# A two-block transformer kernel in split fp32: the order of small steps around its stage changes, and two placing tables moved to GpSimd

## The reference, cut to what matters

```python
# gated linear attention: decays from a low-rank gate
log_a = log_sigmoid(lr @ w_gate2 + b_gate) / 16
cum = cumsum(log_a) in chunks of 64;  last = cum[..., -1, :]
k_dec = k * exp(last - cum);  chunk_decay = exp(last)
state = chunk_decay * state + k_dec^T v;  o = q state

# mixture of experts: a group of 4 experts for each token, then the top 2 of the group
g_idx = argmax(x @ w_group + b_group)
within = top-2 softmax over the 4 experts of that group
y += combine[:, e] * ((silu(x @ w_gate[e]) * (x @ w_up[e])) @ w_down[e])

# differential attention, 8 heads
w = softmax(q1 k1^T * scale + bias) - lam * softmax(q2 k2^T * scale + bias)
o = rms_norm(w @ v) * (1 - lambda_init);  out = o @ w_out
```

## Time and profile before

| what | value |
|---|---|
| median of 3 runs | 1870.49 us (1869.71 to 1872.28) |
| the profiled execution's own time | 1868.49 us |
| its span, first to last instruction | 1866.7 us |
| TensorE busy | 1830.5 us (98%) |
| VectorE busy | 1302.3 us (70%) |
| ScalarE busy | 1013.4 us (54%) |
| GpSimd busy | 107.6 us (6%) |
| mean granted TensorE clock | 0.996 |

### The profile page before, as it was taken

The page is one execution under the profiler, slowest core; times in us unless marked ns, Lnnn a source line. Parts: engine busy times, 40 slices in busy tenths (PEclk is TensorE's granted clock), DMA queues, the critical chain, the costliest instruction groups (busy, mean ns, idle before and its releaser), DMA issues.

```text
span 1866.7 us, 21829 instructions
## 1 busy us (share of the span) xinstructions
PE 1830.5 (98%) x9112; PEld 1531.4 (82%) x9112; DVE 1302.3 (70%) x1333; ACT 1013.4 (54%) x1083; POOL 107.6 (6%) x101
## 2 busy tenths in 40 slices
PE   7999999999999999999999999999999999999998
PEld 6788888887978888887888888888888888888886
DVE  4579999987779899897554677655465546875544
ACT  6447777775646777774443374544344434735431
POOL 1020000001010000000000300100010003020000
PEclk9999999999999999999999999999999999999999
DMA  9447999996446999996555653655565556346541
GB/s 341 153 163 265 357 370 356 359 363 224 137 135 225 359 361 346 375 363 226 188 193 167 195 181 106 207 191 176 191 206 190 176 192 203 134 141 211 190 169 57
DMA packets 220170, 426.57 MB, mean 229 GB/s; under 512 B 7560, under 2 KB 28304, under 8 KB 220064
## 3 DMA queue, kind: packets, MB, share of 16 engines
q1 hardware_dynamic: 214256, 406.93, 63.3%
q0 software_dynamic: 5808, 18.17, 3.2%
HBM read 424.01 MB, written 1.06 MB: 228 GB/s over the span
## 4 chain that ended last, share of the span: by engine, by line
PE 92%; DVE 4%; ACT 2%; DMA 1%; issue 0%; POOL 0%; DVEq 0%; SPq 0%
PE ps L485 26%; PE ps L477 25%; PE ps L480 25%; DVE Wlo L426 2%; PE ps L596 2%; PE ps L469 1%; PE ps L470 1%; PE ps L2526 1%; PE ps L1306 1%; PE ps L1619 1%; PE ps L576 1%; PE ps L575 1%; PE ps L574 1%; ACT Whi L414 1%; PE ps L2427 1%; PE ps L2022 1%
## 5 line engine op out<-in xcount | busy, mean ns | idle before, releaser
L426 DVE TENSOR_TENSOR Wlo<-raw,Whi 128x2048 fp32r<-128x2048 f32 (+2 forms) x387 | 865.6, 2243 | 409.9 <-ACT Whi L414 409.2
L414 ACT ACTIVATE Whi<-raw 128x2048 fp32r<-128x2048 f32 (+2 forms) x393 | 736.0, 1878 | 474.9 <-PE ps L485 469.7
L485 PE MATMUL ps<-Whi,XTl 128*128 128x512 f32 (+2 forms) x1496 | 549.5, 377 | 0.0
L477 PE MATMUL ps<-Whi,XTh 128*128 128x512 f32 (+2 forms) x1368 | 521.0, 381 | 9.4 <-DVE Wlo L426 8.0
L480 PE MATMUL ps<-Wlo,XTh 128*128 128x512 f32 (+2 forms) x1368 | 514.8, 376 | 0.0
L485 PEld LDWEIGHTS ps<-Whi,XTl 128*128 128x128 f32 x1496 | 280.7, 189 | 50.6
L477 PEld LDWEIGHTS ps<-Whi,XTh 128*128 128x128 f32 x1368 | 258.4, 189 | 57.5 <-DVE Wlo L426 8.0
L480 PEld LDWEIGHTS ps<-Wlo,XTh 128*128 128x128 f32 x1368 | 258.4, 189 | 44.6 <-issue 0.3
L477 PE MATMUL ps<-Whi,hTh 128*128 128x512 f32 x352 | 137.8, 391 | 0.0
L485 PE MATMUL ps<-Whi,hTl 128*128 128x512 f32 x352 | 137.1, 390 | 0.0
L480 PE MATMUL ps<-Wlo,hTh 128*128 128x512 f32 x352 | 137.1, 389 | 0.0
(11 more groups left out here) (350 smaller groups left out, 1998.7 us busy)
## 6 DMA issues: line engine op xcount, KB each, us to landing
raw<-in_moe_w_gate SPq DMA_DIRECT2D x64, 1024.0 KB, 5.7
raw<-in_moe_w_up SPq DMA_DIRECT2D x64, 1024.0 KB, 6.4
raw<-in_moe_w_down SPq DMA_DIRECT2D x64, 1024.0 KB, 6.0
raw<-in_ffn_gate SPq DMA_DIRECT2D x44, 1024.0 KB, 5.1
raw<-in_ffn_up SPq DMA_DIRECT2D x44, 1024.0 KB, 5.1
raw<-in_ffn_down SPq DMA_DIRECT2D x40, 1024.0 KB, 5.0
raw<-in_w_in SPq DMA_DIRECT2D x18, 1024.0 KB, 5.2
raw<-in_a_w_in SPq DMA_DIRECT2D x10, 1024.0 KB, 13.2
```

Of the source, the lines that this page charges most:

```text
L414: act.activation(Whi[:, i % NS, 0:m * n], raw[:, i % NR, 0:m * n], ACT.Copy).then_inc(w_rounded, tick(w_rounded, "rounded", i))
L426: dve.tensor_tensor(Wlo[:, i % NR, 0:m * n], raw[:, i % NR, 0:m * n], h.bitcast(f32), ALU.subtract).then_inc(w_rest, tick(w_rest, "rest", i))
L477: pe.matmul(o, xh(k, t), h[:, q, :], start=k == first, stop=False)
L485: x = pe.matmul(o, xl(k, t), h[:, q, :], start=False, stop=k == end)
```

## The change

It has seven parts, none of which changes the number of instructions of TensorE.

1. In the gated linear attention `decays` and `line` change places, on TensorE and on ScalarE: `line` after v1's unit 0, `decays` after its unit 1.
2. In the router's end VectorE takes two of the four gathered parts, then the rest of the first up unit, then the other two parts. Before, it took all four and then the unit.
3. The placing tables of groups 2 and 3 are written by GpSimd, which waits for a new point `chosen` (the mask `gm` is done); VectorE no longer writes them.
4. At the experts' end the add of (group 3, t = 1, first half) goes behind the last `Ygl`, ahead of the overflow branch, and its stats go to the very end, behind the last add.
5. ScalarE copies two of the four parts of the bias table ahead of the turn of X and two behind it (layer 0).
6. In the attention's out product unit 2 takes an `early` callback: it waits for the high half of its input only, runs 8 matmuls, and then waits for the low half.
7. `flip(7)` comes ahead of `values(6)` on TensorE and ScalarE.

```diff
@@ outer_pe
-    def outer_pe(pe, v, name, ready, order=(0, 4), hold=3):
+    def outer_pe(pe, v, name, ready, order=(0, 4), hold=3, early=None):
...
-            use_unit(pe, js[i], t, bs[i % 2][t], xt_h, xt_l, ready, order[0], order[1] + 3)
+            use_unit(pe, js[i], t, bs[i % 2][t], xt_h, xt_l, ready, order[0], order[1] + 3, early=early if i == 2 else None)
@@ gla_pe and gla_act, job v1
             if z == 0:
+                line()
+            if z == 1:
                 decays()
-            if z == 1:
-                line()
@@ gather_two_dve
-    def gather_two_dve(dve, l, p):
-        for kg in range(4):
+    def gather_two_dve(dve, l, p, part=range(4)):
+        for kg in part:
@@ route_dve
-        dve.tensor_tensor(gm[:, :, :], gm[:, :, :], oh[:, :, :], ALU.mult).then_inc(dve_done, tick(dve_done))
+        dve.tensor_tensor(gm[:, :, :], gm[:, :, :], oh[:, :, :], ALU.mult).then_inc(
+            dve_done, tick(dve_done, "chosen", l))
...
-        gather_two_dve(dve, l, 0)
+        gather_two_dve(dve, l, 0, range(2))
         rest_units(dve, jobs["up", l, 0, 0][0])
+        gather_two_dve(dve, l, 0, range(2, 4))
@@ moe_pool
+        P = MAIN[l]
+        pool.wait_ge(*on("chosen", l))
+        for g in range(2, 4):
+            for t in range(2):
+                pool.tensor_scalar(Pm[:, t, g, :], cst[:, C_IOTA:C_IOTA + 128], rank[:, t, g:g + 1], gm[:, t, g:g + 1],
+                                   ALU.is_equal, ALU.mult).then_inc(pool_done, tick(pool_done, P.name, "P", g))
         overflow_pool(pool, l, pool.soon())
@@ moe_act
-            bias_table_act(act)
+            bias_table_act(act, range(2))
         round_units(act, last_unit(v + 1) + 2)
         x_turn_act(act, v + 1, 0)
+        if l == 0:
+            bias_table_act(act, range(2, 4))
@@ moe_dve
         route_dve(dve, l, v)
-        for g in range(2, 4):
-            place_dve(dve, P, g, rank, gm)
...
                     if z == 0 and hf == 1 and g == 3:
-                        for t in range(2):
-                            scatter_dve(dve, P, l, 3, t, 0)
-                            stats_dve(dve, t, 0)
+                        scatter_dve(dve, P, l, 3, 0, 0)
+                        stats_dve(dve, 0, 0)
+        scatter_dve(dve, P, l, 3, 1, 0)
         overflow_dve(dve, l, place)
-        for t in range(2):
-            scatter_dve(dve, P, l, 3, t, 1)
-            stats_dve(dve, t, 1)
-            if t == 0:
-                norm_a_dve(dve, v + 1, 0)
-                norm_b_dve(dve, v + 1, 0)
+        scatter_dve(dve, P, l, 3, 0, 1)
+        stats_dve(dve, 0, 1)
+        norm_a_dve(dve, v + 1, 0)
+        norm_b_dve(dve, v + 1, 0)
+        scatter_dve(dve, P, l, 3, 1, 1)
+        for hf in range(2):
+            stats_dve(dve, 1, hf)
@@ diff_pe
+        def o_early(pe, k, t):
+            if k % 4 == 0:
+                pe.wait_ge(*on("hi", "doT", k // 4, t))
...
-        for z in outer_pe(pe, 3, ("df", "out"), o_ready, hold=2):
-            if z == 0:
+        for z in outer_pe(pe, 3, ("df", "out"), o_ready, hold=2, early=o_early):
+            if z == 0:
+                flip(7)
                 values(6)
-                flip(7)
                 values(7)
@@ diff_act: the same order of flip(7), values(6), values(7)
```

More of the change, by code:

```diff
@@ L1909, in overflow_dve @@
             over_behind(dve, l)
-            for t in range(2):
-                dve.bn_stats(st6[:, t, 0, :], Y[:, t, 0:512]).then_inc(P.dve, tick(P.dve, P.name, "stats"))
+            dve.bn_stats(st6[:, 0, 0, :], Y[:, 0, 0:512]).then_inc(P.dve, tick(P.dve, P.name, "stats"))
             dve.wait_ge(*on(P.name, "stats"))
@@ L1986, in bias_table_pe, with bias_table_act @@
                       start=True, stop=True).then_inc(pe_done, tick(pe_done, "bias", g))
-    def bias_table_act(act):
-        for g in range(4):
+    def bias_table_act(act, part):
+        for g in part:
             act.wait_ge(*on("bias", g))
```

## The result

| | before | changed |
|---|---|---|
| median of the runs beside one another | 1871.38 us (1869.71 to 1876.37, 4 runs) | 1861.28 us (1860.35 to 1861.90, 4 runs) |
| profiled execution, its span | 1868.49, 1866.7 | 1860.80, 1859.0 |

The ratio is 0.9939, with a 95% interval from 0.9922 to 0.9956: 10.1 us faster by the medians, 7.7 by the profiled executions. The prediction was 1865.5 with a range down to 1861.5. The direction is right, the gain is about twice the forecast one, and the time lies 0.2 us under the range.

What follows compares the result with a forecast made beforehand. TensorE bound it, busy 1830.5 of 1866.7 us. Terms -1.49 - 1.75 - 1.2 - 0.3 + 1.3 - 0.9 - 0.7 = -5.0 took 1868.49 to 1863.5; plus 2.0 gave the median, 1865.5, range 1861.5 to 1870.

Steps and rivals of the forecast that it cites:

- In layer 1 Ygl was bound by Ygh, and the matmuls of L1705 cover the norm by some 4 us: 0: Experts' end of layer 1: Ygl waits for Ygh and matmuls hide the norm, so the change wins 0 us there.
- A gap in the instruction stream: Rival, chance 0.08: new layout moves or removes L1705's 2.4 us standstill; up to 4.1 us go or come, 1861.4 or 1869.6.
- Decays and their clock: At the decays: TensorE's wait for la goes, -1.49 us, and the half-clock stretch over L971 goes, -1.75 us.
- The clock takes it back: Rival, chance 0.18: waits go, but half clock stays at the decays and layer 0's new one costs 1.7 us; 1867.6 us.
- Router's end: Router's end of both layers: second gather starts earlier, with comb the next wait; 0.6 us each, -1.2 in all.
- VectorE slows down beside GpSimd: Rival, chance 0.12: GpSimd's tables slow the router's chain on VectorE by 1.1 us, so its 1.2 us are lost; 1867.0 us.
- Experts' end, layer 0, and the clock there: Layer 0's experts' end: shorter wait for Ygl leaves -0.3 us; half clock behind the wait for X costs +1.3 us.
- Attention: In the attention: values(7) no longer waits for dWT(7), -0.9 us; early matmuls cover the out product's low half, -0.7 us.
- The waits only move: Rival, chance 0.09: router and attention stalls reappear at the next semaphore; only the decays' 1.49 us is real; 1869.0 us.
- GpSimd too late: Rival, chance 0.03: the second gather waits for table 3; slower by 3.7 us if one GpSimd instruction takes 3.9 us.
- luck with the clock: Whole run: the profiled execution lay 2.0 us under the median, perhaps by clock luck, so 2.0 us were added.
- the narrow matmuls at 1080: From 1080 to 1088 us: 70 matmuls with few columns ran at full clock, taken as support for the 1.75 us at the decays.

Runs made afterwards that it cites:

- a_no45: The changed kernel without parts 4 and 5 (experts' end as in the kernel before); 1859.97 us, ratio to before 0.9934.
- b_pad1: The kernel before with one more instruction in TensorE's overflow body of layer 1, which is jumped over; 1868.67 us, ratio 0.9992.
- p1: Part 1 alone (decays and line change places) on the kernel before; 1864.35 us, ratio 0.9963.
- b_pad247: The kernel before with 247 more instructions in TensorE's jumped-over overflow body of layer 1; 1867.69 us, ratio 0.9978.
- a_pad253: The changed kernel with 253 more instructions in TensorE's jumped-over overflow body of layer 1; 1864.20 us, ratio to before 0.9965.
- p23: Parts 2 and 3 alone (router's end, two placing tables on GpSimd) on the kernel before; 1870.80 us, ratio 0.9994.
- a_swap: The changed kernel with the second gather ahead of the turn of group 0's placing table; 1861.23 us, ratio to before 0.9941.
- p45: Parts 4 and 5 alone on the kernel before, with 254 jumped-over instructions more to keep its layout; 1871.07 us, ratio 0.9991.
- b_same: The kernel before once more, same build, for a second trace; 1870.96 us, ratio 0.9995.
- p67: Parts 6 and 7 alone (attention's out product and flip(7)) on the kernel before; 1868.01 us, ratio 0.9988.

## Why the prediction was wrong, point by point

**The step that failed** is "In layer 1 Ygl was bound by Ygh, and the matmuls of L1705 cover the norm by some 4 us: 0". In the table that stage is -3.39 us and not 0. The step has two faults. It took the standstill amid L1705 as fixed, and the standstill went with its half clock: -4.1. And the 4 us by which L1705's matmuls covered the norm were that standstill and half clock themselves (8.32 - 4.23 = 4.1). With them gone nothing covered the second stats of part 4: +0.7 (a_no45). The rival "A gap in the instruction stream" named the first mechanism and its price (4.1), but it had a chance of 0.08, half of it for the good side. What stood in its way was a false count: the text ahead of the prediction says that no part changes the number of TensorE's instructions. That holds for its matmuls. It is false for the instructions that only wait, of which three were added, and one is enough (b_pad1, p1). The rival was right as well that it hangs on where the block ends (b_pad247, a_pad253).

**Decays and their clock** (-1.49 - 1.75 = -3.24): -3.41 here and -3.40 in p1. Right, the tiny matmuls of L966 did not hold the clock down. The rival "The clock takes it back" is refuted for this place.

**Router's end** (-1.2): -0.83, in p23 -0.88. The mechanism is right, with comb as the next wait (0.8, as followed) and nothing won at hd; the term was too large by a third. The second gather starts 0.41 us nearer to `gm` and not 0.6 (L1306 at 146.93 - 135.47 = 11.46, before 151.20 - 139.33 = 11.87). Most of the missing 0.2 is `comb`: the prediction had it up to 0.1 earlier, and it came 0.15 later, because VectorE lost 0.37 us beside GpSimd. So the rival "VectorE slows down beside GpSimd" is in part true; it takes some 0.3 of the 1.2 us for both layers, not all.

**Experts' end, layer 0, and the clock there** (-0.3 + 1.3 = +1.0): +0.54 in the changed kernel, +0.99 in a_pad253, +0.97 in a_swap, +1.09 in p45. Ygl waits 1.4 and not 2.1, X 3.0, and the clock falls behind X at 434.4 as foreseen. The sum compared this with an execution in which the old order's fall cost little. The clock falls in this stage in all eight traces with the old order; in three it costs (+0.67, +0.73 and +0.99 in b_same, p23 and a_no45), in five hardly (-0.17 to +0.21). Their mean is +0.3, that of the four with the new order +0.9, so the two terms together measure about 0.6 against a mean execution and 0.5 against the profiled one, not 1.0.

**Attention** (-0.9 - 0.7 = -1.6): -1.63. Right, and the waits did not move on: the rival "The waits only move" falls here and at the decays.

**GpSimd too late**: 4 x 0.83 = 3.3 us of the 11 that it had. Refuted.

**Not in the sum:** +1.64 for a half-clock stretch in the first mixer, where the profiled execution of before had none. b_same, the same build, has two there. The prediction's 2.0 us for "luck with the clock" was this kind of thing: the first trace had three stretches, the second five, and each costs up to 1.7. Also the row of the narrow matmuls at 1080, which the prediction took to say that such work keeps the clock up, says only that it was up: in b_pad1 the same matmuls ran 17 us at 1.2 GHz.

With the missed stage at its -3.4 the sum is -5.0 - 3.4 = -8.4, against 10.1 by the medians. Of the 1.7 us between them, 0.9 is that the median of before was 1870.49 when the prediction was made and 1871.38 with one run more. The other 0.8 is within what the number of half-clock stretches changes from run to run; it stays unassigned. That the median came to lie so near the rival's 1861.4 has some luck in it, since the rival had parts 4 and 5 cost nothing in layer 1.

## What to carry to other kernels

An entry "issue" in the list of waits, soon behind a taken branch and amid equal instructions, was a price of the layout here. Count the instructions that the change adds or drops on that engine, waits and jumped-over bodies included, before calling it fixed; and when a small edit gains more than its own waits, look whether such an entry went. To measure one part of a change, keep the layout with unexecuted instructions, and compare the traces stage by stage at the same matmul: where the clock does not differ, stages repeat to 0.05 us, while the medians of ten runs leave 2 us open. Slack that is read from a timeline with a standstill in it is gone when the standstill goes. And to see whether an engine slows another down, compare the stretch in which both are busy, not the one behind it.

## What the runs showed of the hardware

- Code that is never executed moved the time: one instruction more in a body that is jumped over took 4.1 us out of the stage behind it. The cost is not smooth in the offset: 0 more gave 2.45 us of standstill, 1 and 3 more none, 9 fewer (247 more) 1.29 us. Why one instruction takes all of it away, when the edge should only have moved by one, is not shown; that there is one fetch less then (73 in place of 74), and that the second fetch behind the branch comes 23 to 24 us behind it in place of 9 to 12, would fit code that is placed anew when its start comes close to an edge; no run tests this.
- Behind a hole of 2.2 to 2.6 us in L1705 the clock fell in before, b_same, p23 and p45 and did not in a_pad253 and p67. The same work with the same idle time gets either clock, so a term for the clock is a chance and no amount.
- A half-clock stretch over narrow matmuls lasted 17 us and cost 8.8; one of 6.8 us stands at the decays in b_same and p45 (+1.6). The others lasted 3.4 us, but for the one at the very end of each trace (5.5 to 7.2 us).
- The fetch behind the branch started 2.3 to 2.7 us after it in all 14 traces and took 1.1 to 1.3 us; TensorE stood still only where it reached the end of the block before that.
- GpSimd wrote a 128x128 table with two operands per row in 0.83 us. VectorE's small steps beside four of them took 4.66 us in place of 4.29.
